# Matrix doubling of a chunked delta rule: the inverse's update as one product with the power plus the identity, on one Trainium2 core

## What is computed

```
def step(S, inp):
    r_t, w_t, k_t, v_t, a_t, b_t = inp
    sa = jnp.einsum("bhij,bhj->bhi", S, a_t)
    S = S * w_t[:, :, None, :] + sa[..., None] * b_t[:, :, None, :] + v_t[..., None] * k_t[:, :, None, :]
    y = jnp.einsum("bhij,bhj->bhi", S, r_t)
    return S, y
```

## Time and profile before

| | us |
|---|---|
| median of 3 runs | 1057.34 (1056.35 to 1060.05) |
| the profiled execution | 1058.24 |
| its span, first to last instruction | 1056.5 |
| PE busy | 1041.1 (99%) |
| DVE busy | 680.1 (64%) |
| ACT busy | 503.3 (48%) |
| POOL busy | 356.3 (34%) |

### The profile page before, as it was taken

The page is one execution under the profiler, slowest core; times in us unless marked ns, Lnnn a source line. Parts: engine busy times, 40 slices in busy tenths (PEclk is TensorE's granted clock), DMA queues, the critical chain, the costliest instruction groups (busy, mean ns, idle before and its releaser), DMA issues.

```text
span 1056.5 us, 26383 instructions
## 1 busy us (share of the span) xinstructions
PE 1041.1 (99%) x11199; PEld 981.1 (93%) x11199; DVE 680.1 (64%) x1184; ACT 503.3 (48%) x927; POOL 356.3 (34%) x194
## 2 busy tenths in 40 slices
PE   8999999999999999999999999999999999999998
PEld 8998899998998998899999868989999999999998
DVE  5488788787875666785571691657999989500003
ACT  6453533443434566635462543654666665522232
POOL 4431221321321410255232201353544544444450
PEclk9999999999999999999999999999999999999999
DMA  7321221220223343655154874413334334433222
GB/s 228 89 73 42 61 62 44 61 79 24 61 63 101 113 120 121 200 179 178 53 209 143 266 276 140 145 71 112 104 97 121 104 98 120 159 114 103 81 63 82
DMA packets 164061, 120.44 MB, mean 114 GB/s; under 512 B 5336, under 2 KB 153066, under 8 KB 163433
## 3 DMA queue, kind: packets, MB, share of 16 engines
q1 hardware_dynamic: 159979, 108.08, 33.1%
q10 hardware_dynamic: 3974, 10.80, 3.0%
HBM read 111.04 MB, written 8.30 MB: 113 GB/s over the span
## 4 chain that ended last, share of the span: by engine, by line
PE 84%; DVE 9%; ACT 2%; DMA 2%; issue 2%; POOL 0%; DVEq 0%; SPq 0%; ACTq 0%
PE ps L552 36%; PE ps L1808 15%; PE ps L1164 12%; PE ps L534 10%; PE ps L1875 3%; PE ps L574 2%; DVE conv_y L2849 2%; DVE cache L3285 1%; DMA q_bc<-q_scratch 1%; PE ps L1111 1%; DVE ps L3198 1%; PE ps L600 0%; DMA x_tok<-in_x_prompt_dram 0%; PE ps L1101 0%; DMA w_raw<-in_w_gate_up_dram 0%
## 5 line engine op out<-in xcount | busy, mean ns | idle before, releaser
L1000 POOL TENSOR_TENSOR w_lo<-w_raw,w_hi 128x1024 fp32r<-128x1024 f32 (+2 forms) x83 | 193.4, 2334 | 410.8 <-ACT w_hi L592 358.6
L552 PE MATMUL ps<-h_hi,w_hi 128*128 128x260 f32 x748 | 161.8, 298 | 0.9 <-DVE gate_b L3140 0.6
L552 PE MATMUL ps<-h_hi,w_lo 128*128 128x260 f32 x748 | 150.2, 282 | 0.0
L552 PE MATMUL ps<-h_lo,w_hi 128*128 128x260 f32 x748 | 150.2, 282 | 0.0
L592 ACT ACTIVATE w_hi<-w_raw 128x1024 fp32r<-128x1024 f32 (+2 forms) x95 | 91.2, 965 | 73.0 <-PE ps L552 62.1
L552 PEld LDWEIGHTS ps<-h_hi,w_hi 128*128 128x128 f32 x748 | 115.3, 188 | 10.5 <-issue 4.5
L552 PEld LDWEIGHTS ps<-h_lo,w_hi 128*128 128x128 f32 x748 | 115.1, 188 | 0.0
L552 PEld LDWEIGHTS ps<-h_hi,w_lo 128*128 128x128 f32 x748 | 115.1, 188 | 0.0
L2849 DVE SCALAR_TENSOR_TENSOR conv_y<-glu,prm,conv_y 128x512 f32<-128x512 f32 x120 | 104.0, 867 | 2.5
L3183 DVE TENSOR_TENSOR sq_acc<-sq_acc,sq_tmp 128x264 f32<-128x264 f32 (+2 forms) x35 | 28.6, 817 | 114.6 <-ACT sq_tmp L2708 76.0
L1051 POOL TENSOR_TENSOR w_lo<-w_raw,w_hi 128x512 fp32r<-128x512 f32 x36 | 51.6, 1435 | 98.5 <-ACT w_hi L2591 98.5
(11 more groups left out here) (569 smaller groups left out, 3073.1 us busy)
## 6 DMA issues: line engine op xcount, KB each, us to landing
w_raw<-in_w_gate_up_dram SPq DMA_DIRECT2D x44, 512.0 KB, 4.6
w_raw<-in_w_in_dram SPq DMA_DIRECT2D x38, 512.0 KB, 3.7
cache<-in_cache_mem_k_dram SPq DMA_DIRECT2D x16, 512.0 KB, 6.3
w_raw<-in_w_down_dram SPq DMA_DIRECT2D x16, 512.0 KB, 3.5
cache<-in_cache_mem_v_dram SPq DMA_DIRECT2D x14, 512.0 KB, 7.0
w_raw<-in_w_k_dram SPq DMA_DIRECT2D x8, 512.0 KB, 3.7
w_raw<-in_w_v_dram SPq DMA_DIRECT2D x8, 512.0 KB, 3.7
w_raw<-in_w_out_dram SPq DMA_DIRECT2D x8, 512.0 KB, 3.8
```

The lines of the kernel that those rows point to most:

```text
L552: mm = nc.tensor.matmul(ps[:, 2 * s + a, 0:width], w[:, k, :], x[:, x0 + k, a * width:(a + 1) * width], start=(first and k == 0 and n == 0 ...
L1000: pool.tensor_tensor(lo[:, 0:kts], w_raw[:, b % RAW_SLOTS, 0:kts], hi[:, 0:kts].bitcast(F32), ALU.subtract).then_inc(w_lo_ready, 1)
```

## The change

The identity product and its accumulation go. DVE makes a new tile `at_one` = AT + identity, from `big` and `stack_id` in SBUF, and the update of the inverse is one product with it: X <- (A^(2^d) + 1) X. The product of AT with PW becomes one of its own. As `at_one` needs the evicted AT of both banks, ACT evicts both banks alone in `dbl0` to `dbl4`, in one instruction, and DVE waits for ACT's count (`step_a`) before the add. `dbl5` is evicted by both engines as before, only XI. `at_one` lies in the place of `tmp1`, which the pair's preparation uses before and after the lockstep. In `dbl0` the two products swap banks.

```
--- before.py
+++ after.py
@@ -225,6 +225,7 @@
     bh_fm = buf("bh_fm", [P, NC, HS])
     kh_fm = tmp2[:, 0:T].rearrange("p (c n) -> p c n", n=HS)
     v_chunks = xs[:, 2, 0:T].rearrange("p (c n) -> p c n", n=HS)
+    at_one = tmp1[:, 0:T].rearrange("p (c n) -> p c n", n=HS)
 
 
     AT, XI, PW, RB, BH, AR, AKV = (slice(HS * j, HS * (j + 1)) for j in range(7))
@@ -1236,8 +1237,8 @@
                 elif name == "dbl0":
                     for c, n, i, odd, h in four:
                         r, j = rows(h, odd, False), 2 * i + h
-                        small(ps[r, base, HS * j:HS * (j + 1)], big[r, n, AT], big[r, n, PW])
-                        mm = small(ps[r, base + 1, HS * j:HS * (j + 1)], big[r, n, PW], big[r, n, AT])
+                        small(ps[r, base, HS * j:HS * (j + 1)], big[r, n, PW], big[r, n, AT])
+                        mm = small(ps[r, base + 1, HS * j:HS * (j + 1)], big[r, n, AT], big[r, n, PW])
                 elif name.startswith("dbl"):
                     d = int(name[3:])
                     for i in range(2):
@@ -1246,11 +1247,10 @@
                             for n, h, r, to in some:
                                 small(region(to, i, h, 0, HS), big[r, n, PW], big[r, n, AT])
                         for n, h, r, to in some:
-                            width = 1 if d >= 4 else 2
-                            small(region(to, i, h, HS, HS * (1 + width)), big[r, n, AT], big[r, n, HS:HS * (1 + width)],
-                                  stop=False)
-                        for n, h, r, to in some:
-                            mm = small(region(to, i, h, HS, 2 * HS), stack_id[r, :], big[r, n, XI], start=False)
+                            mm = small(region(to, i, h, HS, 2 * HS), at_one[r, n, :], big[r, n, XI])
+                        if d < 4:
+                            for n, h, r, to in some:
+                                mm = small(region(to, i, h, 2 * HS, 3 * HS), big[r, n, AT], big[r, n, PW])
                 elif name == "apply":
                     for c, n, i, odd, h in four:
                         r, to = rows(h, odd, True), rows(h, odd, False)
@@ -2045,10 +2045,13 @@
                 elif name == "akv":
                     ins = go(pairs(big[:, cs, AKV]), both(base, 0, HS), ACT.Copy)
                 elif name == "dbl0":
-                    ins = go(big[:, cs, AT], ps[:, base + 1, 0:4 * HS].rearrange("p (c n) -> p c n", c=4), ACT.Copy)
+                    ins = go(big[:, cs, 0:4 * HS].rearrange("p c (j n) -> p j c n", n=HS)[:, 0:3:2],
+                             ps[:, base:base + 2, 0:4 * HS].rearrange("p j (c n) -> p j c n", c=4), ACT.Copy)
+                elif name == "dbl5":
+                    ins = go(big[:, odds, XI], ps[:, base + 1, :].rearrange("p (i n) -> p i n", i=2)[:, :, XI], ACT.Copy)
                 elif name.startswith("dbl"):
-                    a, b = {"dbl4": (0, 2 * HS), "dbl5": (HS, 2 * HS)}.get(name, (0, 3 * HS))
-                    ins = go(big[:, odds, a:b], ps[:, base + 1, :].rearrange("p (i n) -> p i n", i=2)[:, :, a:b], ACT.Copy)
+                    a, b = 0, (2 if name == "dbl4" else 3) * HS
+                    ins = go(pairs(big[:, cs, a:b]), both(base, a, b), ACT.Copy)
                 elif name == "apply":
                     ins = go(pairs(big[:, cs, 5 * HS:7 * HS]), both(base, 0, 2 * HS), ACT.Copy)
                 elif name == "h":
@@ -2848,6 +2851,11 @@
                 else:
                     link_v(stt(conv_y[:, p, 0:T], src, w, conv_y[:, p, 0:T], ALU.mult, ALU.add))
 
+            def one_added(p, k, cs):
+
+                dve.wait_ge(step_a, emptied("a", p, k + 1))
+                return tt(at_one[:, cs], big[:, cs, AT], stack_id[:, :].unsqueeze(1).to_broadcast([P, 4, HS]), ALU.add)
+
             def step_out(p, k):
                 name, q, engines = STEPS[k]
                 if "v" not in engines:
@@ -2867,11 +2875,12 @@
                     m = mask_t[:, 0, :].unsqueeze(1).unsqueeze(1).to_broadcast([P, 2, 2, HS])
                     ins = tt(pairs(big[:, cs, AT]), both(base, 0, HS), m, ALU.mult)
                 elif name == "dbl0":
-                    ins = V.tensor_copy(big[:, cs, PW], ps[:, base, 0:4 * HS].rearrange("p (c n) -> p c n", c=4))
+                    ins = one_added(p, k, cs)
+                elif name == "dbl5":
+                    ins = V.tensor_copy(big[:, 4 * q:4 * q + 4:2, XI],
+                                        ps[:, base, :].rearrange("p (i n) -> p i n", i=2)[:, :, XI])
                 elif name.startswith("dbl"):
-                    a, b = {"dbl4": (0, 2 * HS), "dbl5": (HS, 2 * HS)}.get(name, (0, 3 * HS))
-                    ins = V.tensor_copy(big[:, 4 * q:4 * q + 4:2, a:b],
-                                        ps[:, base, :].rearrange("p (i n) -> p i n", i=2)[:, :, a:b])
+                    ins = one_added(p, k, cs)
                 elif name == "y":
                     dve.wait_ge(step_a, emptied("a", p, N_STEPS))
                     for h in range(2):
```

1 line of the change is left out of this document (added).

## The result

The changed kernel takes 1064.26 us (median of 7, 1062.89 to 1066.17), the kernel before 1057.44 (7 runs, 1056.35 to 1061.79): a ratio of 1.0054, interval [1.004, 1.0068]. It is slower by 6.8 us, forecast were 1.4, and 1064.3 lies above the range's end of 1061.8. The profiled execution took 1066.17, its span 1064.4: 7.9 more than the span before.

The account below looks back on a forecast made before the run. PE's own instructions were taken to set the time. Per pair, -2.14 saved and +0.20, +0.27, +1.95, +0.10 lost gave +0.38, or +1.4 us in all: 1058.7 from 1057.34, range 1052.4 to 1061.8.

Parts of the forecast that it names:

- The savings of the products: PE's lockstep, `dbl1` to `dbl5`: narrower and fewer products save 2.14 us a pair, 8.6 us in four pairs.
- The rival of weight loads: `dbl1` to `dbl3`: weight loads bound the narrow products, so these save nothing; +4.4 us, 1061.7; chance 0.05.
- The wide eviction: ACT's 768 wide eviction of both banks: 0.81 us, bounds 0.60 and 1.19.
- The meeting with POOL: `dbl4` to `dbl5`: POOL's `w_lo` holds DVE's SBUF add until 4.36 us after `dbl4` starts; PE stalls 1.95 us.
- The add's tail: `dbl4`: held add ends 0.24 us after POOL, 0.19 of its start hidden; by the page, the full 0.42 after POOL.
- The sum: All four pairs: +0.39 us in three, +0.24 in the last, passed on by the PE-bound rest: +1.4 us.
- the last part: What the changed timeline would show: add of some 2 us in `dbl4`, PE waits some 9 us, and what would upset this.
- The direction: Whole kernel: slower by 1.4 us, 1058.7 against 1057.34.
- the forecast's own case: Whole kernel with POOL holding the add: 1058.7 us, within 1056.9 to 1061.2; chance 0.68.
- `dbl3`: Step from `dbl3` to `dbl4`: 0.40 us saved by narrower products, less a 0.27 us stall carried in from `dbl2`.
- the second add's stall: `dbl2` to `dbl3`, second half: DVE's second add, behind a tap, is ready at 3.46 against 3.19, stalling PE 0.27 us.

Follow-up runs that it names:

- the longer idle time: Add from PSUM, PE waiting before `dbl5` for POOL's `w_lo`; against that kernel, one slice moved from `dbl4` to the pair's end: 1067.59 us.

## Why the prediction was wrong

*Right.* The savings of the products: `dbl1` -0.18 to -0.21 (forecast -0.20), `dbl2` -0.41 where no gap fell. The rival of weight loads is out: the 96 instructions of `dbl2` take 1.63 us from first start to last end in the pairs without a gap (2.03 before), under the 1.75 that would have decided for it. The wide eviction at 0.81 against 0.81 worked out of the earlier trace rows. The meeting with POOL: the add ends at 177.89, 0.30 after POOL's 177.59 (forecast 0.24), PE starts at 177.93; `dbl4` grew by 1.48 (forecast 1.48), in the last pair by 1.33. The add's tail is between the two that were weighed: nothing hidden would have been 0.42. The Trainium skill's "whole instruction" (SBUF — State Buffer, "SBUF: two separate sides") is right about the lock and some 0.1 us too long here. The Trainium skill has the lock meet a VectorE operation with two SBUF inputs, and the add with one operand in PSUM, not held (0.44), agrees.

*The step that failed* is "The sum": "the rest of the kernel, bound by PE, passes the shift on". PE doesn't come out of a 1.9 us wait as it went in. In three of four pairs its granted clock was 0.50 behind it, which cost 1.5 us a pair, 4.5 in all by the steps, and the sum had no term for it, though the last part names "if PE's clock fell in the 2 us waits". It was listed as something that could upset the size and given neither price nor chance, so the range ended at 1061.8. A rival could have been priced from a row: the earlier trace rows has the products of `apply` at 1.10, and half the clock would add as much again, 4.4 us in four pairs, 1063.1. For a chance the trace before had one row, near its start, where PE had waited 1.50 us for `x_tok` until 8.98:

```profile
10.00:14.00 4.00, 4.00 (x23) 3.87 (x21) 3.95 (x10) 4.00 (x9) 3.74 (x3) 0.57 0.36 101
```

The clock was at half behind that wait too, from 10.3 to 13.7 us. One row can't say how often this happens: in the changed kernel's profile the same wait lasts 2.24 us, and the clock behind it stays full. In the locksteps of the trace before PE never waits over 0.8 us. The direction was right, but a forecast of 1.4 us in a range with both signs says little by that.

*A slip in the bounds*: the parts named for the forecast's own case add up to -1.6 and +2.8 us, 1057.1 to 1061.5, and not to the 1056.9 to 1061.2 given. The measured time lies outside either.

*A term mis-sized*: `dbl3`. Forecast -0.13, measured -0.03 in the pairs without gaps: 0.1 a pair, 0.4 in all. If all of it lies in the second add's stall, that was 0.36 and not 0.27.

*Not seen*: that the lockstep has short gaps at fixed counts of PE's instruction stream. Taking out 64 matmuls and their loads a pair moves the rest of the program against those places. Against the same steps without a gap, pair 3 lost 1.7 us in three steps before and 1.6 in two after, but pair 2 lost nothing before and 0.8 after. The earlier trace rows were read from pair 2 alone, where no gap was to be seen; pair 3 had them.

*The remainder.* Forecast 1.4, clock 4.5, gaps and `dbl3` 1.1: 7.05 in the locksteps of the two profiles. The medians differ by 6.8; that the two figures are so close is in part luck, as the gaps and the rest of the span vary by 1 to 2 us from one execution to the next.

## To carry to other kernels

Ask of every new wait of the critical engine how long it idles and not only how late it is. Here waits of 1.0 to 1.4 us in the lockstep cost their length in every profile. Waits of 1.5 to 1.9 us were followed by 1.5 us more in three of eight places, waits of 2.2 to 2.4 us by 1.5 to 2.8 us more in three of four. So a wait that can't be avoided is worth filling or shortening, even by 0.7 us.

An operand's place can be worth more than a removed instruction. With the identity added to the power in PSUM instead of in SBUF the same idea was faster than the kernel before (1054.6), and with ScalarE taken off the path of `dbl4` and the taps placed for it 1052.6.

Once the lockstep is tight, PE's instruction fetch can be what stops it: from 0 to 7 us of gaps stood in four locksteps. That depends in part on where the blocks fall, which is luck of the layout, and it has to be measured anew after each edit.

## What was not expected of the hardware

- PE's granted clock went to 0.50 after waits of 1.7 to 1.9 us (3 of 4) and 2.2 to 2.35 us (3 of 4), and stayed at 1.00 after waits of 1.0 to 1.2 us (4 of 4), 1.4 us (4 of 4) and, in one profile, of 1.5 to 1.8 us (4 of 4). Which of equal waits is spared differs: one of 1.73 us was hit, one of 1.89 and one of 2.35 were not.
- The wait for `x_tok` at 9 us shows the same without any edit to it: half the clock behind 1.50, 1.57, 1.76, 1.97 and 2.26 us, full behind 2.24, 2.32 and 2.46. Over all 14 profiles the clock fell at 11 of 21 idle times of 1.5 to 2.5 us and at none of 18 of 0.9 to 1.45 us. It also fell once with no such idle time: with the 16 small products in front, PE was busy with products of 4 columns from 7.2 to 11.1 us, and the clock was at half from 10.4 to 17.3.
- The fall need not wait for PE to go on. In the change's second pair PE was back at 177.93 and the clock still full to 179. In the first pair of the longer idle time PE was back at 105.24, and 104 to 106 us already reads 0.73, so the clock fell some 0.3 us before.
- A block crossing in PE's instruction stream is visible where PE takes 254 instructions in 3.5 us, and not outside the locksteps. A gap ended 1.24 to 1.61 us after the end of a 16 KB instruction packet, 43 times of 43.
- An SBUF add held by POOL ends 0.30 us after it, where it takes 0.42 alone; the same add with one operand in PSUM is not held (0.44 each beside POOL).
